# Other constants for the planner that orders the work of five engines in a hybrid attention block

## The reference

```python
proj = rmsnorm(x, pre_norm) @ w_in                  # 2048 x 6664 with the gate
o_a = diff(a_q, a_k, a_v)      # softmax(q0 k0 + bias) - lam * softmax(q1 k1 + bias), times v
o_b = stick(sb_q, sb_k, sb_v)  # exp(log_sigmoid(z) + sum of log_sigmoid(-z) of later keys), times v
o_c = forget(f_q, f_k, f_v)    # softmax(q k + c[q] - c[k]), times v
o_m = mem(m_q, mem keys, mem values)
y = concat(o_a, o_b, o_c, o_m) * silu(gate)
out = x + rmsnorm(y @ w_out, post_norm)
```

## Time and profile before

| what | value |
| --- | --- |
| median of 3 runs | 2732.6 us (2725.76 to 2734.64) |
| the profiled execution, own time | 2734.1 us |
| its span, first to last instruction | 2732.2 us |
| mean granted TensorE clock | 0.973 |
| PE busy | 2448.7 us (90%) |
| DVE, ACT, POOL busy | 1803.1, 1616.6, 1340.9 us (66, 59, 49%) |
| hardware DMA queue | 334.83 MB, 62.7% of 16 engines |

### The profile page before, as it was taken

The page is one execution under the profiler, slowest core; times in us unless marked ns, Lnnn a source line. Parts: engine busy times, 40 slices in busy tenths (PEclk is TensorE's granted clock), DMA queues, the critical chain, the costliest instruction groups (busy, mean ns, idle before and its releaser), DMA issues. The chain is left out here.

```text
span 2732.2 us, 73492 instructions
## 1 busy us (share of the span) xinstructions
PE 2448.7 (90%) x27422; PEld 1669.4 (61%) x27422; DVE 1803.1 (66%) x4993; ACT 1616.6 (59%) x4437; POOL 1340.9 (49%) x2128
## 2 busy tenths in 40 slices
PE   5799999988899999888999998889999997599998
PEld 4576666665666666666766766567666665444443
DVE  7658988765479887665699976646998775311111
ACT  5457765567667755576677555766785557511121
POOL 6414457766434576674245766752456677400000
PEclk9899999999999999999999999989999999799999
DMA  6346874498758943898589537994886368963331
GB/s 204 91 99 116 148 141 98 83 172 152 160 103 142 158 105 79 159 161 158 102 152 154 118 77 148 156 169 92 157 143 126 82 128 151 187 207 97 104 108 47
DMA packets 942750, 357.38 MB, mean 131 GB/s; under 512 B 768292, under 2 KB 927148, under 8 KB 942380
## 3 DMA queue, kind: packets, MB, share of 16 engines
q1 hardware_dynamic: 935800, 334.83, 62.7%
q0 software_dynamic: 6592, 17.83, 2.4%
HBM read 89.22 MB, written 35.23 MB: 46 GB/s over the span
## 5 line engine op out<-in xcount | busy, mean ns | idle before, releaser
L1507 POOL TENSOR_TENSOR rows<-rows 128x512 f16<-128x512 f32 (+3 forms) x864 | 861.1, 1010 | 808.3 <-ACT rows L1442 804.2
L1271 PE MATMUL job<-wt,big 128*128 128x128 f16 x10752 | 672.9, 221 | 9.3 <-DVE planes L1518 4.5
L1271 PE MATMUL job<-big,wt 128*128 128x512 f16 x2688 | 662.7, 384 | 18.5 <-DVE planes L1518 6.7
L1271 PEld LDWEIGHTS job<-wt,big 128*128 128x128 f16 x10752 | 630.0, 99 | 59.6 <-DVE planes L1518 11.4
L1442 ACT CAST rows<-rows 128x512 f16<-128x512 f32 (+3 forms) x864 | 465.1, 547 | 254.7 <-DVE rows L1589 123.4
L1332 PE MATMUL mixed<-values,rows 128*128 128x64 f16 (+1 forms) x8544 | 446.2, 202 | 119.0 <-DMA rows<-rows 89.2
L1332 PEld LDWEIGHTS mixed<-values,rows 128*128 128x128 f16 x8544 | 391.4, 100 | 254.6 <-DMA rows<-rows 132.3
L1454 ACT ACTIVATE rows<-rows,neg_max 128x512 f32<-128x512 f32 (+3 forms) x704 | 447.0, 637 | 89.4 <-DVE neg_max L1564 88.4
L1556 DVE TENSOR_SCALAR_CACHE_REDUCE rows<-scores 128x512 f32<-128x512 f32 (+3 forms) x704 | 400.0, 588 | 148.0 <-POOL rows L1507 125.4
L1317 PE MATMUL scores<-stack 128*128 128x512 f16 (+3 forms) x1600 | 438.1, 351 | 54.5 <-DVE rows L1556 44.3
L1271 PEld LDWEIGHTS job<-big,wt 128*128 128x128 f16 x2688 | 249.0, 99 | 277.9 <-issue 20.6
(11 more groups left out here) (160 smaller groups left out, 3000.8 us busy)
## 6 DMA issues: line engine op xcount, KB each, us to landing
stack<-planes SPq DMA_DIRECT2D x160, 192.0 KB
ws<-w_in SPq DMA_DIRECT2D x56, 512.0 KB, 4.6
y_halves<-y_out_halves SPq DMA_DIRECT2D x64, 256.0 KB, 3.3
rows<-rows SPq DMA_TRANSPOSE x864, 3.3
rows<-x SPq DMA_DIRECT2D x16, 512.0 KB, 5.7
temps<-w_out POOLq DMA_DIRECT2D x64, 128.0 KB, 3.2
out_weight_halves<-temps POOLq DMA_DIRECT2D x64, 128.0 KB, 3.6
planes<-y_halves SPq DMA_DIRECT2D x8, 1024.0 KB, 8.7
```

Source lines behind the costliest of these rows:

```text
L1271: last = nc.tensor.matmul(dst, lhs, rhs, start=(k0 == 0 and q == 0), stop=(k1 == KT and q == len(pairs) - 1))
L1507: nc.gpsimd.tensor_tensor(halves_of(tau, 1, w), scored(plan.chunk_at(g, m, k0), 0, w), halves_of(tau, 0, w), ALU.subtract).then_inc(low_po ...
```

## The change

Only constants of the planner change: the believed latency of a hop between engines, the ranks on PE, ACT, DVE and SP, three of the four shares of projection done ahead, the slack and the penalty. No instruction is added or removed; the sequence on the engines is what can differ. The sizes of the rings stay.

```diff
-HOP, SAME = 0.08, 0.03
+HOP, SAME = 0.152, 0.03
 RANK = {
-    "pe": {"gate": -0.56896, "y": 0.65716, "mix": 2.26812, "score": 3.66995, "project": 6.06207},
-    "act": {"take": -0.56306, "beta": 0.18730, "job": 5.24904, "stick": 7.44050, "convert": 7.47892,
-            "hi": 7.82832, "exp": 8.61381},
-    "dve": {"low": 3.02114, "weigh": 3.66090, "lo_dve": 5.58491, "widen": 5.68258, "post": 5.97032,
-            "near": 6.20571, "combine": 6.74865, "copy": 7.57977, "scan": 8.13881},
+    "pe": {"gate": -0.69350, "mix": 0.82372, "score": 2.95609, "y": 4.31887, "project": 6.43835},
+    "act": {"take": 1.10697, "beta": 4.34092, "job": 5.24904, "stick": 7.34182, "hi": 7.82832,
+            "convert": 7.82832, "exp": 8.11520},
+    "dve": {"low": -0.76237, "weigh": 0.36094, "combine": 4.51969, "post": 5.42085, "near": 5.51271,
+            "copy": 6.20571, "lo_dve": 6.68090, "widen": 7.54196, "scan": 8.13881},
     "pool": {"root": 0.00000, "lo": 1.00000, "wo": 2.00000},
-    "sp": {"pairs": 0.50000, "turn": 0.80000, "stacks": 0.90000, "strip": 1.00000, "sums": 2.00000,
-            "store": 3.00000, "near_in": 4.00000},
+    "sp": {"turn": -0.62632, "strip": -0.24996, "near_in": 2.26686, "store": 3.63016, "sums": 4.97585,
+            "pairs": 7.55752, "stacks": 8.51997},
 }
-AHEAD = {0: 0.10000, 1: 0.51500, 2: 0.58645, 3: 0.72022}
-SLACK, LATE = 3.83945, 5.18846
+AHEAD = {0: 0.74778, 1: 0.51500, 2: 0.48997, 3: 0.66327}
+SLACK, LATE = 3.79816, 7.63635
```

## The result

| | before | after |
| --- | --- | --- |
| median of 4 runs | 2732.4 us | 2698.7 us (2697.1 to 2700.6) |
| ratio, 95% interval | 1 | 0.988 (0.9865 to 0.9895) |
| profiled execution, span | 2732.2 us | 2698.7 us |
| first matmul of the output product | 2387 us | 2353 us |

The change makes the kernel 34 us faster where 13 us had been forecast: the right side, but little over a third of the size. The time lies inside the range given, 2688 to 2751, nearer to rival B's 2690 than to the forecast's 2720. Measured again later, beside one of the experiments, the ratio was 0.9873 (0.9856 to 0.9889).

The account below looks back on a forecast made before the run. The prediction took PE's 224.8 us idle in the main block, uneven and largest in forget, as all an order can win. Terms 11 + 2 + 8 - 7 - 1 = 13 us faster gave 2720 us, range 2688 to 2751.

Parts of the forecast that it names:

- rival B: Forget stretches: turns first on SP bring forget closer to its chain (22 us), clock 8 us more; 2690, chance 0.15.
- What bounds the kernel: Main block: PE's 224.8 us idle, and clock lost beside them, are all an order can win; forget is short of work.
- The shares: Projection done ahead: forget's lower share leaves 4.1 us a lane for forget, 8 us faster, 16 at most.
- diff's share: Projection done ahead for diff: its lower share moves 6.9 us from stick to diff, worth nothing.
- Mem's share: Projection done ahead for mem: the higher share moves nothing, as PE already fills holes with it; 0 us.
- The hop: Main block: larger hop adds margin, shortening PE's waits for transposes by 11 us and for banks by 2.
- rival A: Whole plan: nothing moves, a wrong hop only shifts the waits elsewhere; 2732, chance 0.24.
- SP, 7 us slower: Unit starts on SP: turns ahead of stack loads delay these by half a transpose at 11 starts, 7 us slower.
- rival C: Unit starts on SP: stack loads starve, 28 us lost and gains halved to 10; 2750, chance 0.20.
- DVE, ACT, y, 1 us: Ranks on DVE, ACT and PE: widen behind copies costs 1 us; the other swaps, y's included, 0.
- Its own tests: Signs: transpose waits 70 to 80 us, PE busy 7 us lower in stick, 4 higher in forget, score gap near 13.
- The sum: Whole kernel: 11 + 2 + 8 - 7 - 1 = 13 us faster, 2721, given as 2720.

Follow-up runs that it names:

- b_ahead: Kernel before with only the changed shares done ahead, slack and penalty: 2729.0 us, ratio 1.0002 to the kernel before.
- a_ahead: Changed kernel with shares, slack and penalty put back: 2744.8 us, ratio 1.0055 to the kernel before.
- a_share0: Changed kernel with mem's share put back from 0.748 to 0.10: 2696.4 us, ratio 0.9902 to the kernel before.
- a_sp: Changed kernel with the ranks on SP put back: 2698.7 us, ratio 0.9901 to the kernel before.
- a_share2: Changed kernel with diff's share put back from 0.490 to 0.586: 2737.6 us, ratio 1.0042 to the kernel before.
- c_mean: Kernel before with hop 0.04 and other constants searched for a short order at mean latencies: 2736.0 us, ratio 1.004 to the kernel before.
- a_hop: Changed kernel with the hop alone put back to 0.08: 2745.9 us, ratio 1.0062 to the kernel before.
- b_sp: Kernel before with only the changed ranks on SP: 2786.7 us, ratio 1.0221 to the kernel before.
- a_ranks: Changed kernel with the ranks on PE, ACT and DVE put back: 2724.4 us, ratio 0.998 to the kernel before.
- a_pe: Changed kernel with the ranks on PE alone put back: 2709.9 us, ratio 0.9946 to the kernel before.
- b_hop: Kernel before with the hop alone raised from 0.08 to 0.152: 2752.9 us, ratio 1.0088 to the kernel before.

## Why the prediction was wrong

**What bounds the kernel** held: all of the 34 us came out of the main block, 20 as idle time and about 10 through the clock, with 4 us of busy time unexplained, and the idle part came out of forget stretches, which the prediction had called the regime with PE short of other work.

**The shares** are the step that failed, by size and by mechanism. It had 8 us, 16 at most, from 4.1 us a lane left for forget by forget's share, and "nothing" for diff's share. Measured: 11 to 12 us a lane, in lanes two to four; forget took it in without becoming longer. The first lane got none (by the plan, 47.5 us of forget's projection is done at its last diff score) and became no shorter, 563 us from its first stick score to the next lane's before and 566 after, where the second and third lanes went from 558 to 547 and 545. (The fourth is 7 us shorter to the end of the block, and the other 6 of the 34 us stand before the first stick score.) And the carrier is diff's share: put back alone it costs 39 us, forget's, the one that was given 8, 17 (24 by the ratios). The step read a share as an amount to be moved. It is a lower mark, and what counts is how much PE takes as filler beyond it: the shares move nothing with the old hop and ranks (b_ahead) and 46 us with the new (a_ahead). Mem's share was rightly given nothing (a_share0: level).

**The clock** stood only in rival B, and 10 of the 34 us came through it. The sum had no such term, and it is no rare one: over the nineteen kernels PE's busy time in the main block lies between 2037 and 2088 us, for the same matmuls, and goes with the time at 1.2 GHz, 85 to 165 us. B's mechanism, a more filled forget and less time at the low clock, is what happened, but not its price (22 us by a closer chain: the forget stretches shown stayed at 137 and 136 us) nor its cause on SP (a_sp: SP's ranks do nothing here). In a_share2's forget stretch the granted clock is 0.98 while the wide filler lasts and 0.85 after it, when PE is busy 54 of 73 us. The Trainium skill (TensorE: Matmul & The Clock Gate, HAM oscillation) has the rule that the low clock comes back where matmuls stand in short runs between DMA waits; these two rows agree with it.

**The hop** was 11 + 2 us. The waits for transposes fell by 5.7 us in one profile of the changed kernel and by 13.7 in the other, so the size of the wait's change may have been right; what it is worth was not. Alone, the margin takes 10.8 us off these waits and makes the kernel 24 us slower. So the term took a local wait for the bound. I read the margin in another way: with it, a short plan is one that stays short when hops and landings come late. Replayed at 0.152 the changed order is 38 us shorter than the one before, and c_mean, short only at 0.08, is slow on the chip; beyond that this reading is not shown. a_hop, with 0.08 and the rest of the change, is 17 us slower than the kernel before, so the old value is not what such a plan needs, and rival A falls.

Nor is 0.152 simply the truer mean. The prediction had one hop for that; the trace of before has more. Where the receiver stood waiting, a `lo` of 512 columns starts 0.70 us after its `hi` did (median of 324), which the planner at 0.08 puts at 0.68; from `weigh` to the next sigmoid it is 0.77 us against 0.77, from `lo` to `copy` 1.28 against 1.29. Transposes land 3.6 us after their issue in the mean, where the planner has 4.0. So 0.08 is not too short. The Trainium skill's 50 to 100 ns (Advanced Engine Details and Errata, Network/Comms: reading a semaphore from a sequencer) agrees with the one hop of 70 ns; the inference that a plan with a longer hop must be worse is what failed.

**SP, 7 us slower**: nothing (a_sp). The gap where forget starts is the prediction's own test for rival C. PE's timeline there in the changed kernel, as in the earlier trace rows:

```profile
1082.76 0.49 PE L1317 MATMUL scores<-near,ident_b 128*128 128x256 bf16 x3
...
1096.67 0.22 PE L1317 MATMUL scores<-stack 128*128 128x128 f16 x1
```

From 1083.25 to 1096.67 it is 13.4 us, where it was 12.7: no starving. The danger was real, though: 58 us in the old order (b_sp).

**DVE, ACT, y, 1 us**: as a set worth 26 us (a_ranks), PE's ranks alone 11 (18 by the ratios, a_pe), where the prediction had 0 for y. What hides y's place was named wrongly: y ahead of mix goes along with 37 us of projection taken in stick instead of 30.

**Its own tests**: PE's waits for transposes were to fall to 70 to 80 us and mostly outside forget (83.5 and 75.5 us in the two profiles, so one inside and one not; in the first, forget's four stretches keep their 30.9 us, so the fall is outside them as forecast); PE's busy sum in stick to fall by 7 us a lane and in forget to rise by 4 (second lane: 4.3 lower and 5.2 higher, with 4.4 us lower in diff: the right signs, with diff as giver too); the gap at forget's start near 13 us (13.4, right).

**The sum** added parts that don't add. Alone they measure +24, 0, +22 and +58 us (sum 104 slower), together -34.

## What to carry to other kernels

When fixed streams are written out by a planner, replay each order with later latencies than the mean: in this kernel that ranked eighteen orders better than the plan's own length did, and the profile's largest wait did not tell the gain. Judge constants only as a set. Take two profiles of one kernel before reading anything into a wait that changed by a few us. Where one stage leaves the bounding engine short of work, look for filler that earlier stages consume without need, and check it by counting its instructions in each stretch. The parts of this change could not be priced one by one from the trace of before.

## What was not expected of the hardware

PE's busy time for identical work varied by 51 us (2037 to 2088) over these orders, along with the time at 1.2 GHz: 86 us in the changed kernel, 165 us in b_sp. And the time that PE waited for transposes, which land in 2.3 to 7.4 us, says little about an order: it is 78 to 89 us in before, after, b_hop, a_hop and b_sp, which are up to 88 us apart, and 64 to 102 us over all twenty profiles, with a correlation of only 0.63 with the ratio measured.
